# Two-block layer on one core: one feed-forward round in pairs of units over four PSUM banks, and one unit half in products of 256 columns

## The chip, the cores and the metric

One Trainium2 chip; the program uses 1 of its cores. The metric is the device time of the whole kernel in microseconds, one launch. The kernel before took 1955.97 us (median of 3 runs, 1955.89 to 1957.13).

## The reference

The input `x` is 512 tokens of 1024 numbers. It passes through two blocks. The first has sparse attention beside a linear recurrence and a gated feed-forward part. The second has two layers; what a layer of it computes at its end is what the change touches:

```python
for l in range(DEPTH_2):                                  # 2 layers
    ...
    x = x + jnp.einsum('bse,ed->bsd', mixed, w_o[l])
    h = rmsnorm(x, mlp_norm[l])
    u = jnp.square(jax.nn.relu(jnp.einsum('bsd,df->bsf', h, w_ff1[l])))   # 1024 -> 4096
    x = x + jnp.einsum('bsf,fd->bsd', u, w_ff2[l])                        # 4096 -> 1024
return rmsnorm(x, final_norm)
```

All tensors are float32.

## The kernel before, in words

Activations lie transposed in SBUF: 8 tiles of 128 features by 512 tokens. A matrix product with a weight is cut into **units**: a unit makes 128 output features for all 512 tokens, in one PSUM bank, from 8 tiles of 128 input features. To keep the accuracy of float32 with the faster float32r products, weights and activations are each split into a high and a low part, and each of the 8 steps `k` is three products of 512 columns: high weight by high activation, high weight by low activation, low weight by high activation (L1621, L1622, L1623). A unit is therefore 24 products, each with a weight load of its own. 280 units of the kernel run in this form, numbered through; unit n uses bank `accs[n % 2]`.

The program is one list of items (`whole()`), and every engine walks the same list and does its own part of each item, in the order of the list. What happens for unit n:

- SyncE starts the load of its 512 KB into `raw` (L671), one of 3 slots, as soon as the unit that had the slot has been split.
- ScalarE makes the high part with one copy of 128 x 1024 (`split_hi`, L778). It does so two units ahead: in the item `mmA` of unit n it splits unit n + 2.
- GpSimd makes the low part in 4 pieces of 128 x 256 (`split_lo`, L737). It waits for the high part and then runs as early as it may. `whi` and `wlo` are rings of 4 slots.
- TensorE has two items for a unit, `mmA` (k 0 to 3) and `mmB` (k 4 to 7). `mmA` waits for the high part, for half of the low part, and for the accumulator to be free (semaphore `acc`: every unit up to n - 2 has been read); `mmB` waits for the rest of the low part.
- VectorE reads the finished bank. In a unit of the first weight (`w_ff1`) this is the item `relu`: VectorE multiplies the bank by the norm (L1105), makes relu and square (L1458), ScalarE copies the result to its high part `Uh` (L1013), VectorE makes the low part `Ul` (L1461). In a unit of the second weight (`w_ff2`) it is `resid`: one VectorE addition into `xT` (L1210).

The feed-forward part of a layer of the second block runs in 4 rounds of 1024 hidden features, `ffn_round(r, last)`: 8 units of `w_ff1`, each followed by its `relu`, then 8 units of `w_ff2`, each followed by its `resid`. The first unit of `w_ff2` waits for `Ul` tile by tile (`first`). In layer 0 round 0 is units 135 to 150, **round 1 is units 151 to 166**, round 2 is units 167 to 182.

The wait on the accumulator and the order of ScalarE's work are these lines:

```python
if begun("unit", -1):
    pe.wait_ge(sems["acc"], at("unit", -1))      # mmA of unit n: units 0 to n - 2 were read
...
for ahead in item[1].get("splits", (2,)):        # ScalarE, mmA of unit n
    split_hi(ahead)
```

Of the kernel before, what the change touches and what calls it, by code (L numbers as in the profile page):

```python
# [52 lines left out]
def shape_constants():  # L53
# [43 lines left out]
    "xin": dict(S_fill=1, S_act=1, xh=1, xl=1), "xsq": dict(), "xsum": dict(x_sum=1), "warm": dict(), "split": dict(), "loads": dict(), "cmpc": dict(cmp_c=1),  # L97
    "prep": dict(sq=1, xh=1, xl=1),
    "norm": dict(M_fill=1, M_act=1, rstd=1), "norm0": dict(M_fill=1, M_act=1, rstd=1),
    "mmA": dict(), "mmB": dict(unit=1), "mmK": dict(),  # L100
    "resid": dict(acc=1),

    "evc": dict(acc=1, cmp_t=1),
# [132 lines left out]
def mm(unit):  # L236
    return [("mmA", unit), ("mmB", unit)]
# [171 lines left out]
def block2(layer, behind=0):  # L409
    s = [("lay",)]  # L410

    def u(col, **kw):
        return unit("w_in_2", col, "h", k0=8 * layer, **kw)

    cols = {"sq": 0, "sk": 512, "sv": 1024, "dq": 1536, "dk": 2048, "dv": 2560}
    attn = []
    for kind, j, *rest in periods(ORDER2, LAST2):
        if kind in ("mmA", "mmB"):
            begins = j == 0 and rest[0] == "sq"
            attn.append((kind, u(cols[rest[0]] + 128 * j, first=begins)))  # L420
            if begins and kind == "mmB":
                attn.append(("norm",))
        elif kind == "on2":
            attn.append(("on2", j, 4 + j))
        elif kind in ("vt", "vt2", "dfr", "rope"):
            attn.append((kind, *rest))
        else:
            attn.append((kind, j, *rest))
    order = produced(attn)
    w_o = [unit("w_o_2", 128 * c, "u", order, first=(c < 4), k0=8 * layer, bank=c) for c in range(KC)]  # L430
    attn = with_early(attn, w_o)
    s += attn
    s += outputs(w_o, attn, "cur", 8)

    def ffn_round(r, last):
        out = []
        for c in range(8):
            out += mm(unit("w_ff1_2", 1024 * r + 128 * c, "h", first=(c == 0 and r == 0), k0=8 * layer))
            out += ([("norm",)] if c == 0 and r == 0 else []) + [("relu", c)]
        for c in range(KC):  # L440
            out += mm(unit("w_ff2_2", 128 * c, "u", first=(c == 0), k0=32 * layer + 8 * r)) + [("resid", c)]
            if last:
                out.append(("prep", c, ("cur", c)))
        return out

    s += ffn_round(0, False) + ffn_round(1, False)
    if layer == 0:
        return s + ffn_round(2, False) + ffn_round(3, True)
    s += [("gload",)] + ffn_round(2, False)
    last = units_of(s) + behind + 8  # L450

    def down(n):
        return unit("w_ff2_2", P * ((last + n) % RING if n < RING else n), "u", k0=32 * layer + 24)

    for c in range(8):
        s += mm(unit("w_ff1_2", 3072 + 128 * c, "h", k0=8 * layer, splits={5: (2, 3), 6: (3,), 7: (3,)}.get(c, (2,))))
        if c == 7:
            s.append(("wn", down(0), 0))
        s.append(("relu", c))
        s += [("nat", c)] if c < 6 else [("nat", 6), ("nat", 7)] if c == 7 else []  # L460
    s += [("wn", down(n), n) for n in range(1, 8)]
    s += [("grp", b, 0) for b in range(NB)]
    for b in range(NB):
        s += [("grp", b, 1), ("fin", b)]
    return s
# [49 lines left out]
def build(nc, dram, out):  # L515
    sched = whole()
    with ExitStack() as ctx:
# [129 lines left out]
        def _(sp):  # L647
# [30 lines left out]
            def stage(w, item):  # L678
# [17 lines left out]
                elif kind == "loads":  # L696
                    n = item[1]
                    if n == 0:
                        sp.dma_start(cst[:, EARLY:LATE], dram["consts"][:, EARLY:LATE]).then_inc(sems["ld_const2"], 16)
                    v, a = sems[f"ld_cmp{n}"], "kv"[n]  # L700
                    sp.dma_start(w1[n], dram[f"cmp_{a}_w1"][0].rearrange("(a p) c -> p a c", p=P)).then_inc(v, 16)
                    sp.dma_start(w2[n], dram[f"cmp_{a}_w2"][0]).then_inc(v, 16)
                elif kind == "mmA":
                    fetch(item[1], 0)
                elif kind == "mmP" and item[3] == 0:
                    fetch(item[1], item[2])
                elif kind == "rotary":
                    c0 = CONST_AT["cos"][0]
                    sp.wait_ge(sems["T_fill"], at("T_fill"))
                    sp.wait_ge(sems["S_fill"], at("S_fill"))  # L710
                    sp.dma_start(cst[:, c0:c0 + 2 * T], dram["consts"][:, c0:c0 + 2 * T]).then_inc(sems["ld_rotary"], 16)
                elif kind == "gload":
                    sp.wait_ge(sems["acc"], at("acc", -20))
                    g = dram["final_norm_2"]
                    sp.dma_start(gainT, bass.AP(g.tensor, g.offset, [[0, P], [1, D]])).then_inc(sems["ld_gain"], 16)
                elif kind == "wn":
                    fetch(item[1], item[2])
                elif kind == "fin":
                    b = item[1]
                    for h, y in enumerate(("y0", "y1")):  # L720
                        sp.wait_ge(sems[y], b + 1)
                        sp.dma_start(x_out[:, b, T * h:T * h + T], ob[:, b, T * h:T * h + T]).then_inc(sems["outd"], 16)
# [6 lines left out]
        def _(pool):  # L729
# [16 lines left out]
            def stage(w, item):  # L746
                if item[0] == "mmA":
                    split_lo(0)
                elif item[0] == "mmP" and item[3] == 0:
                    split_lo(item[2])  # L750
                elif item[0] == "wn":
# [15 lines left out]
        def _(act):  # L767
# [16 lines left out]
            def stage(w, item):  # L784
# [36 lines left out]
                elif kind == "mmA":  # L821
                    for ahead in item[1].get("splits", (2,)):
                        split_hi(ahead)
                elif kind == "mmP":
                    if item[3] == 0 and item[2] < 2:
                        split_hi(2 + item[2])
# [262 lines left out]
        def _(dve):  # L1089
# [4 lines left out]
            def acc():  # L1094
                return accs[:, (w.base["unit"] - 1) % 2]

            def gain(where):
                kind, n = where
                return vec[:, n:n + 1] if kind == "vec" else cur[:, n:n + 1]
# [22 lines left out]
            def stage(w, item):  # L1122
# [82 lines left out]
                    STT(Xl[:, c], xT[:, c], gain(g), Xh[:, c].bitcast(F32), ALU.mult, ALU.subtract).then_inc(sems["xl"], 1)  # L1205
                elif kind == "resid":
                    c = item[1]
                    dve.wait_ge(sems["unit"], at("unit"))
                    y = M[:, :] if item[2:] and item[2] == IN_M else TT[:, item[2] - 2] if item[2:] and item[2] > 1 else acc()
                    TTn(xT[:, c], xT[:, c], y, ALU.add).then_inc(sems["acc"], 1)  # L1210
                    dve.wait_ge(sems["acc"], at("acc", 1))
                elif kind == "evc":
# [241 lines left out]
                    TTn(Ul[:, item[1]], tu, Uh[:, item[1]].bitcast(F32), ALU.subtract).then_inc(sems["ul"], 1)  # L1454
                    dve.wait_ge(sems["ul"], at("ul", 1))
                elif kind == "relu":
                    scaled(tg)
                    STT(tu, tg, 0.0, tg, ALU.max, ALU.mult).then_inc(sems["u_new"], 1)  # L1458
                    dve.wait_ge(sems["u_new"], at("u_new", 1))
                    dve.wait_ge(sems["uh"], at("uh", 1))  # L1460
# [90 lines left out]
        def _(pe):  # L1551
# [10 lines left out]
            def stage(w, item):  # L1562
# [41 lines left out]
                elif kind in ("mmA", "mmB"):  # L1604
# [10 lines left out]
                    for i, k in enumerate(ks):  # L1615
# [2 lines left out]
                        if u["first"]:  # L1618
                            pe.wait_ge(sems[ready], at(ready, i + 1 - len(ks) + u.get("early", 0)))
                        y = accs[:, n % 2]  # L1620
                        mmul(y, whi[:, slot, k], xh[:, k], start=(i == 0), stop=False)  # L1621
                        mmul(y, whi[:, slot, k], xl[:, k], start=False, stop=False)  # L1622
                        last = mmul(y, wlo[:, slot, k], xh[:, k], start=False, stop=(i == len(ks) - 1))  # L1623
                    if kind == "mmB":
                        last.then_inc(sems["unit"], 1)
                elif kind == "mmP":
                    _, u, ahead, lo, hi = item
                    n = w.base.get("unit", 0) + ahead
# [301 lines left out]
```

## Time and profile before

| | |
|---|---|
| median of 3 runs | 1955.97 us |
| profiled execution, first to last instruction (its own time: no other is recorded) | 1953.9 us |
| median less that span | 2.1 us |
| TensorE busy with products | 1923.8 us, 98% |
| TensorE weight loads (they run beside products) | 1510.5 us, 77% |
| VectorE busy | 916.7 us, 47% |
| ScalarE busy | 834.5 us, 43% |
| GpSimd busy | 881.6 us, 45% |
| mean granted TensorE clock | 0.999 of full speed |
| DMA | 86 GB/s in the mean |

The span is the time from the first to the last instruction of the profiled execution. The busy time of products counts each from its start to its modelled end, 0.39 us for 512 columns, so that neighbours overlap; what one product costs is the distance between two starts, called the pitch here.

### The profile page before, as it was taken

To read this page: it belongs to the slowest core of one execution; us is meant where nothing else is said; L and a number is where in the kernel's file an instruction comes from. 1 tells how busy PE (TensorE), PEld (TensorE's weight loads), DVE (VectorE), ACT (ScalarE), POOL (GpSimd) and SP (SyncE) were. 2 spreads that over 40 slices of the span, in tenths; PEclk is the share of its full clock that TensorE was granted. 3 is DMA by queue.
4 is the path that set the end of the run, shared out by engine and by line. 5 is a ranking of instruction groups with operands and counts; after the bars stand their busy time and mean duration, and the time that the engine had idled before them with its cause. 6 is when DMAs were issued, how large, how long until landed. Compare 5 with 4: busy or idle time off the path is not lost. (4 is left out here: it accounts for less than half of the span.)

```text
span 1953.9 us, 25592 instructions
## 1 busy us (share of the span) xinstructions
PE 1923.8 (98%) x9150; PEld 1510.5 (77%) x9150; DVE 916.7 (47%) x1420; ACT 834.5 (43%) x1269; POOL 881.6 (45%) x1188
## 2 busy tenths in 40 slices
PE   9999999999999999999999999999999999999998
PEld 7866766788888887777688888887777688888887
DVE  5487877432241346777541313133777643222132
ACT  4466555543242345555532223134555542222233
POOL 4322221456456465343355455454443355454543
PEclk9999999999999999999999999999999999999999
DMA  8211111233234233222134233333222223243322
GB/s 234 65 44 44 34 44 33 87 106 110 84 89 119 76 96 99 75 66 75 48 107 116 78 108 97 87 97 95 78 66 76 65 85 110 86 119 86 109 86 76
DMA packets 318100, 168.77 MB, mean 86 GB/s; under 512 B 15028, under 2 KB 313367, under 8 KB 317847
## 3 DMA queue, kind: packets, MB, share of 16 engines
q1 hardware_dynamic: 314432, 162.38, 28.9%
q10 hardware_dynamic: 3542, 4.76, 1.0%
q8 instruction: 74, 1.21, 0.3%
q14 instruction: 52, 0.42, 0.1%
HBM read 160.29 MB, written 2.10 MB: 83 GB/s over the span
## 5 line engine op out<-in xcount | busy, mean ns | idle before, releaser
L737 POOL TENSOR_TENSOR wlo<-raw,whi 128x256 fp32r<-128x256 f32 x1164 | 865.2, 775 | 1042.2 <-ACT whi L778 1042.2
L1621 PE MATMUL accs<-Xh,whi 128*128 128x512 f32 x1448 | 581.3, 401 | 0.1
L1623 PE MATMUL accs<-Xh,wlo 128*128 128x512 f32 x1448 | 565.1, 390 | 0.0
L1622 PE MATMUL accs<-Xl,whi 128*128 128x512 f32 x1448 | 563.9, 389 | 0.0
L778 ACT ACTIVATE whi<-raw 128x1024 fp32r<-128x1024 f32 x291 | 307.7, 1061 | 267.6 <-PE accs L1623 218.5
L1621 PEld LDWEIGHTS accs<-Xh,whi 128*128 128x128 f32 x1448 | 272.1, 188 | 58.6 <-issue 3.7
L1623 PEld LDWEIGHTS accs<-Xh,wlo 128*128 128x128 f32 x1448 | 271.8, 188 | 58.4
L1622 PEld LDWEIGHTS accs<-Xl,whi 128*128 128x128 f32 x1448 | 272.4, 188 | 56.1 <-issue 3.6
L1621 PE MATMUL accs<-Uh,whi 128*128 128x512 f32 x744 | 289.7, 389 | 0.8 <-DVE xT L1210 0.8
L1622 PE MATMUL accs<-Ul,whi 128*128 128x512 f32 x744 | 289.4, 389 | 0.0
L1623 PE MATMUL accs<-Uh,wlo 128*128 128x512 f32 x744 | 289.4, 389 | 0.0
L1210 DVE TENSOR_TENSOR xT<-xT,accs 128x512 f32<-128x512 f32 x101 | 69.4, 687 | 338.1 <-PE accs L1623 333.9
L1105 DVE TENSOR_TENSOR W<-accs,rstd 128x512 f32<-128x512 f32 x123 | 85.1, 692 | 261.8 <-PE accs L1623 244.0
L1013 ACT ACTIVATE Uh<-W 128x512 fp32r<-128x512 f32 x86 | 54.4, 632 | 313.8 <-DVE W L1458 272.0
L1621 PEld LDWEIGHTS accs<-Uh,whi 128*128 128x128 f32 x744 | 139.7, 188 | 30.9 <-issue 1.6
L1623 PEld LDWEIGHTS accs<-Uh,wlo 128*128 128x128 f32 x744 | 139.7, 188 | 29.1
L1622 PEld LDWEIGHTS accs<-Ul,whi 128*128 128x128 f32 x744 | 139.7, 188 | 28.7
L1461 DVE TENSOR_TENSOR Ul<-W,Uh 128x512 fp32r<-128x512 f32 x64 | 45.1, 705 | 49.3 <-ACT Uh L1013 49.3
L1510 DVE TENSOR_TENSOR_SCAN W<-W 128x128 f32<-128x128 f32 (+3 forms) x64 | 58.3, 910 | 3.1 <-ACT W L1029 0.9
L836 ACT ACTIVATE sq<-xT 128x512 f32<-128x512 f32 x40 | 25.4, 634 | 78.8 <-DVE xT L1210 72.5
L1001 ACT ACTIVATE W<-W 128x512 f32<-128x512 f32 x22 | 13.9, 633 | 102.0 <-DVE W L1110 102.0
L1458 DVE SCALAR_TENSOR_TENSOR W<-W 128x512 f32<-128x512 f32 x64 | 47.2, 738 | 2.2
(303 smaller groups left out, 1913.8 us busy)
## 6 DMA issues: line engine op xcount, KB each, us to landing
raw<-in_w_ff_dram SPq DMA_DIRECT2D x128, 512.0 KB
raw<-in_w_in_dram SPq DMA_DIRECT2D x71, 512.0 KB
raw<-in_w_gate_up_dram SPq DMA_DIRECT2D x44, 512.0 KB
raw<-in_w_down_dram SPq DMA_DIRECT2D x16, 512.0 KB
raw<-in_w_o_dram SPq DMA_DIRECT2D x16, 512.0 KB
px<-W ACTq DMA_DIRECT2D x64, 64.0 KB, 2.0
raw<-in_w_down_dram SPq DMA_DIRECT2D x8, 384.0 KB
W<-in_x_dram SPq DMA_DIRECT2D x4, 512.0 KB, 6.1
```

What stands on the lines that cost most here:

```text
L737: pool.tensor_tensor(lo[:, ks], raw[:, unit_no % RAW, ks], hi[:, ks].bitcast(F32), ALU.subtract).then_inc(sems["wlo"], 1)
L778: A(XhW[:, ahead - RING] if ahead >= RING and late else whi[:, slot], raw[:, n % RAW], ACT.Copy).then_inc(sems["whi"], 1)
L836: A(sq[:, :], xT[:, c], ACT.Square).then_inc(sems["sq"], 1)
L1013: A(Uh[:, c], tu, ACT.Copy).then_inc(sems["uh"], 1)
L1105: TTn(dst, accs[:, (w.base["unit"] - 1 - back) % 2], rstd[:, :], ALU.mult).then_inc(sems["acc"], 1)
L1210: TTn(xT[:, c], xT[:, c], y, ALU.add).then_inc(sems["acc"], 1)
L1458: STT(tu, tg, 0.0, tg, ALU.max, ALU.mult).then_inc(sems["u_new"], 1)
L1461: TTn(Ul[:, item[1]], tu, Uh[:, item[1]].bitcast(F32), ALU.subtract).then_inc(sems["ul"], 1)
L1510: dve.tensor_tensor_scan(back, back, backwards(R[:, h, :]), 0.0, ALU.add, ALU.add).then_inc(sems["dve"], 1)
L1621: mmul(y, whi[:, slot, k], xh[:, k], start=(i == 0), stop=False)
L1622: mmul(y, whi[:, slot, k], xl[:, k], start=False, stop=False)
L1623: last = mmul(y, wlo[:, slot, k], xh[:, k], start=False, stop=(i == len(ks) - 1))
```

## The change

1. `ffn_round` gets an argument `woven`; it is true for round 1 of layer 0 only. In that round two units are one item `mm2`. Its products alternate: step k of unit n, step k of unit n + 1, for each of the three kinds of product. The units of the round take four banks in turn, `accs[0]`, `accs[1]`, `S[0]`, `S[1]` (unit n has bank n % 4); `S` belongs to the attention and lies idle here. The two `relu` or `resid` of a pair follow both units in the list.
2. An `mm2` waits at its start for the high and low parts of both units, and for `acc` up to unit n - 3 (two pairs back); the first pair of the round waits until all units before it were read.
3. In an `mm2`, SyncE fetches both units, ScalarE splits the units n + 2 and n + 3, and GpSimd makes the low parts of n and n + 1.
4. In round 2 of layer 0, unit 170 (c = 3) runs its steps k 4 to 7 as `mmH`: each product of 512 columns becomes two of 256 columns into the two halves of the same bank, each with its own weight load.

```diff
-    def ffn_round(r, last):
+    def ffn_round(r, last, woven=False):
         out = []
+        if woven:
+            for c in range(0, 8, 2):
+                out.append(("mm2", unit("w_ff1_2", 1024 * r + 128 * c, "h", k0=8 * layer),
+                            unit("w_ff1_2", 1024 * r + 128 * c + 128, "h", k0=8 * layer), c == 0))
+                out += [("relu", c, 1), ("relu", c + 1, 0)]
+            for c in range(0, KC, 2):
+                out.append(("mm2", unit("w_ff2_2", 128 * c, "u", first=(c == 0), k0=32 * layer + 8 * r),
+                            unit("w_ff2_2", 128 * c + 128, "u", first=(c == 0), k0=32 * layer + 8 * r), False))
+                out += [("resid", c, 0, 1), ("resid", c + 1, 0, 0)]
+            return out
         for c in range(8):
-            out += mm(unit("w_ff1_2", 1024 * r + 128 * c, "h", first=(c == 0 and r == 0), k0=8 * layer))
+            u = unit("w_ff1_2", 1024 * r + 128 * c, "h", first=(c == 0 and r == 0), k0=8 * layer)
+            if r == 2 and c == 3 and layer == 0:
+                u["loose"] = True
+            out += [("mmA", u), ("mmH", u)] if r == 2 and c == 3 and layer == 0 else mm(u)
...
-    s += ffn_round(0, False) + ffn_round(1, False)
+    s += ffn_round(0, False) + ffn_round(1, False, layer == 0)
...
+                elif kind == "mm2":                      # SyncE
+                    fetch(item[1], 0)
+                    fetch(item[2], 1)
...
+                elif item[0] == "mm2":                   # GpSimd
+                    split_lo(0)
+                    split_lo(1)
...
+                elif kind == "mm2":                      # ScalarE
+                    split_hi(2)
+                    split_hi(3)
...
+            def bank4(n):                                # VectorE
+                return (accs[:, 0], accs[:, 1], S[:, 0], S[:, 1])[n % 4]
...
                 elif kind == "resid":
                     c = item[1]
-                    dve.wait_ge(sems["unit"], at("unit"))
-                    y = M[:, :] if item[2:] and item[2] == IN_M else TT[:, item[2] - 2] if item[2:] and item[2] > 1 else acc()
+                    back = item[3] if item[3:] else 0
+                    dve.wait_ge(sems["unit"], at("unit", -back))
+                    y = bank4(at("unit", -1 - back)) if item[3:] else M[:, :] if item[2:] and item[2] == IN_M else TT[:, item[2] - 2] if item[2:] and item[2] > 1 else acc()
...
                 elif kind == "relu":
-                    scaled(tg)
+                    if item[2:]:
+                        dve.wait_ge(sems["unit"], at("unit", -item[2]))
+                        dve.wait_ge(sems["rstd"], at("rstd"))
+                        TTn(tg, bank4(at("unit", -1 - item[2])), rstd[:, :], ALU.mult).then_inc(sems["acc"], 1)
+                        dve.wait_ge(sems["acc"], at("acc", 1))
+                    else:
+                        scaled(tg)
...
+                elif kind == "mm2":                      # TensorE
+                    _, u, u1, begins = item
+                    n = w.base["unit"]
+                    banks = (accs[:, 0], accs[:, 1], S[:, 0], S[:, 1])
+                    pe.wait_ge(sems["whi"], n + 2)
+                    pe.wait_ge(sems["wlo"], LO_PARTS * (n + 2))
+                    pe.wait_ge(sems["acc"], n if begins else n - 2)
+                    pe.wait_ge(sems["S_act"], at("S_act"))
+                    pe.wait_ge(sems["S_dve"], at("S_dve"))
+                    xh, xl, ready = (Xh, Xl, "xl") if u["x"] == "h" else (Uh, Ul, "ul")
+                    for k in range(KC):
+                        if u["first"]:
+                            pe.wait_ge(sems[ready], at(ready, k + 1 - KC))
+                        for a in range(2):
+                            mmul(banks[(n + a) % 4], whi[:, (n + a) % RING, k], xh[:, k], start=(k == 0), stop=False)
+                        for a in range(2):
+                            mmul(banks[(n + a) % 4], whi[:, (n + a) % RING, k], xl[:, k], start=False, stop=False)
+                        for a in range(2):
+                            last = mmul(banks[(n + a) % 4], wlo[:, (n + a) % RING, k], xh[:, k], start=False, stop=(k == KC - 1))
+                            if k == KC - 1:
+                                last.then_inc(sems["unit"], 1)
+                elif kind == "mmH":
+                    u = item[1]
+                    n = w.base["unit"]
+                    slot = n % RING
+                    pe.wait_ge(sems["wlo"], LO_PARTS * (n + 1))
+                    for k in range(KC // 2, KC):
+                        for h in range(2):
+                            t = slice(T // 2 * h, T // 2 * h + T // 2)
+                            y = accs[:, n % 2, t]
+                            mmul(y, whi[:, slot, k], Xh[:, k, t], start=False, stop=False, skip_group_check=True)
+                            mmul(y, whi[:, slot, k], Xl[:, k, t], start=False, stop=False, skip_group_check=True)
+                            last = mmul(y, wlo[:, slot, k], Xh[:, k, t], start=False, stop=(k == KC - 1), skip_group_check=True)
+                    last.then_inc(sems["unit"], 1)
```

The first place is ScalarE at the start of round 1: `whi<-raw` is the high part of a weight (L778, L797 in the change), `Uh<-W` the copy in a `relu` (L1013, L1035 in the change). Before:

```order
L1013 ACTIVATE Uh<-W 128x512
L778 ACTIVATE whi<-raw 128x1024 x9
L1013 ACTIVATE Uh<-W 128x512
L778 ACTIVATE whi<-raw 128x1024
L1013 ACTIVATE Uh<-W 128x512
```

And in the change:

```order
L1035 ACTIVATE Uh<-W 128x512
L797 ACTIVATE whi<-raw 128x1024 x10
L1035 ACTIVATE Uh<-W 128x512 x2
L797 ACTIVATE whi<-raw 128x1024 x2
L1035 ACTIVATE Uh<-W 128x512 x2
```

One high part after each `relu` became two high parts after each two `relu`: behind the `relu` of the first pair (units 151, 152) stand the high parts of units 155 and 156.

The second place is TensorE at the same point of the program, from the last step of unit 150 to the second step of the pair 151 and 152. Before:

```order
L1623 MATMUL accs<-Uh,wlo 128x512
L1621 MATMUL accs<-Xh,whi 128x512
L1622 MATMUL accs<-Xl,whi 128x512
L1623 MATMUL accs<-Xh,wlo 128x512
L1621 MATMUL accs<-Xh,whi 128x512
```

And in the change, where lines L1673, L1675 and L1677 are the three products of `mm2`:

```order
L1656 MATMUL accs<-Uh,wlo 128x512
L1673 MATMUL S<-Xh,whi 128x512
L1673 MATMUL accs<-Xh,whi 128x512
L1675 MATMUL S<-Xl,whi 128x512
L1675 MATMUL accs<-Xl,whi 128x512
L1677 MATMUL S<-Xh,wlo 128x512
L1677 MATMUL accs<-Xh,wlo 128x512
L1673 MATMUL S<-Xh,whi 128x512
```

The number of products of the round is the same, 384; each is now followed by one into another bank. Of this pair, unit 151 goes to `S[1]` and unit 152 to `accs[0]`, the bank of unit 150.

## Rows read from the trace of the kernel before

**Rows 1.** The page: span, and busy time and instructions of each engine

```profile
span 1953.9 us, 25592 instructions
PE 1923.8 (98%) x9150; PEld 1510.5 (77%) x9150; DVE 916.7 (47%) x1420; ACT 834.5 (43%) x1269; POOL 881.6 (45%) x1188
```

**Rows 2.** Round 1: stretch, busy PE, PEld, DVE, ACT, POOL, clock, DMA share, GB/s

```profile
1078.30:1165.30 87.00, 87.00 (x386) 72.06 (x385) 22.12 (x32) 21.95 (x24) 45.13 (x64) 1.00 0.34 97
```

**Rows 3.** Timeline of TensorE (start us, us): from unit 150 into unit 151

```profile
1078.17 0.39 PE L1623 MATMUL accs<-Uh,wlo 128*128 128x512 f32 x1
1078.40 0.39 PE L1621 MATMUL accs<-Xh,whi 128*128 128x512 f32 x1
...
1078.40 0.19 PEld L1622 LDWEIGHTS accs<-Xl,whi 128*128 128x128 f32 x1
```

**Rows 4.** Timeline of TensorE: a change of bank in the attention of layer 1

```profile
1552.40 0.40 PE L1648 MATMUL accs<-Uh,wlo 128*128 128x512 f32 x1
1552.63 0.40 PE L1646 MATMUL TT<-Uh,whi 128*128 128x512 f32 x1
```

**Rows 5.** Timeline of VectorE: last `resid` of round 0, first `relu` of round 1

```profile
1078.67 0.69 DVE L1210 TENSOR_TENSOR xT<-xT,accs 128x512 f32<-128x512 f32 x1 [4.75 <-PE accs L1623]
1084.10 0.69 DVE L1105 TENSOR_TENSOR W<-accs,rstd 128x512 f32<-128x512 f32 x1 [4.74 <-PE accs L1623]
1084.82 0.69 DVE L1458 SCALAR_TENSOR_TENSOR W<-W 128x512 f32<-128x512 f32 x1
1086.28 0.69 DVE L1461 TENSOR_TENSOR Ul<-W,Uh 128x512 fp32r<-128x512 f32 x1 [0.77 <-ACT Uh L1013]
```

**Rows 6.** Timeline of ScalarE in round 1

```profile
1085.54 0.63 ACT L1013 ACTIVATE Uh<-W 128x512 fp32r<-128x512 f32 x1 [11.32 <-DVE W L1458]
1086.21 1.06 ACT L778 ACTIVATE whi<-raw 128x1024 fp32r<-128x1024 f32 x1
...
1124.29 2.01 ACT L778 ACTIVATE whi<-raw 128x1024 fp32r<-128x1024 f32 x2
```

**Rows 7.** Timeline of GpSimd in round 1

```profile
1087.35 2.83 POOL L737 TENSOR_TENSOR wlo<-raw,whi 128x256 fp32r<-128x256 f32 x4 [10.23 <-ACT whi L778]
1125.43 8.40 POOL L737 TENSOR_TENSOR wlo<-raw,whi 128x256 fp32r<-128x256 f32 x12 [2.61 <-ACT whi L778]
```

**Rows 8.** Timeline: TensorE held by VectorE's read of a bank, layer 1

```profile
1565.27 1.41 DVE L1210 TENSOR_TENSOR xT<-xT,accs 128x512 f32<-128x512 f32 x2 [1.12 <-PE accs L1648]
...
1566.94 0.47 PE L1621 MATMUL accs<-Uh,whi 128*128 128x512 f32 x1 [0.39 <-DVE xT L1210]
1567.25 0.40 PE L1622 MATMUL accs<-Ul,whi 128*128 128x512 f32 x1
```

**Rows 9.** Timeline: TensorE held by a high part, after eight transposes

```profile
1902.72 1.03 PE L1559 MATMUL S<-cst,xT 128*128 128x128 f32 x8
1902.92 1.06 ACT L778 ACTIVATE whi<-raw 128x1024 fp32r<-128x1024 f32 x1 [1.69 <-PE accs L1623]
...
1904.03 0.50 PE L1897 MATMUL accs<-whi,Uh 128*128 128x512 f32 x1 [0.28 <-ACT whi L778]
```

**Rows 10.** Timeline of round 0: VectorE and GpSimd at the same time

```profile
1003.22 1.18 DVE L1458 SCALAR_TENSOR_TENSOR W<-W 128x512 f32<-128x512 f32 x1
1001.72 3.28 POOL L737 TENSOR_TENSOR wlo<-raw,whi 128x256 fp32r<-128x256 f32 x4 [4.97 <-ACT whi L778]
```

**Rows 11.** A weight's DMA in round 1: its issue; stretches with the columns of rows 2

```profile
1090.26 5.83 SPq L671 DMA_DIRECT2D raw<-in_w_ff_dram  x2
...
1090.20:1091.20 1.00, 1.00 (x6) 0.84 (x5) 0.72 (x2) 0.21 (x1) 0.00 (x0) 1.00 0.00 0
1091.20:1093.80 2.60, 2.60 (x13) 2.15 (x12) 0.69 (x1) 1.48 (x2) 1.01 (x2) 1.00 0.70 201
```

**Rows 12.** Groups by form (count | busy us, mean ns of one | idle): transposes, products of 64 rows

```profile
L1559 PE MATMUL S<-cst,xT 128*128 128x128 f32 x32 | 4.6, 272 | 0.0
L1854 PE MATMUL TT<-W 64*128 64x512 f32 x32 | 9.0, 641 | 0.0
```

More of the change, by code:

```diff
@@ L99 @@
     "norm": dict(M_fill=1, M_act=1, rstd=1), "norm0": dict(M_fill=1, M_act=1, rstd=1),
-    "mmA": dict(), "mmB": dict(unit=1), "mmK": dict(),
+    "mmA": dict(), "mmB": dict(unit=1), "mmK": dict(), "mm2": dict(unit=2), "mmH": dict(unit=1),
     "resid": dict(acc=1),
@@ L1620, in stage @@
                         y = accs[:, n % 2]
-                        mmul(y, whi[:, slot, k], xh[:, k], start=(i == 0), stop=False)
-                        mmul(y, whi[:, slot, k], xl[:, k], start=False, stop=False)
-                        last = mmul(y, wlo[:, slot, k], xh[:, k], start=False, stop=(i == len(ks) - 1))
+                        loose = "loose" in u
+                        mmul(y, whi[:, slot, k], xh[:, k], start=(i == 0), stop=False, skip_group_check=loose)
+                        mmul(y, whi[:, slot, k], xl[:, k], start=False, stop=False, skip_group_check=loose)
@@ L1624, in stage @@
+                        last = mmul(y, wlo[:, slot, k], xh[:, k], start=False, stop=(i == len(ks) - 1), skip_group_check=loose)
                     if kind == "mmB":
                         last.then_inc(sems["unit"], 1)
+                elif kind == "mm2":
[32 more added lines that the diff above has]
+                    last.then_inc(sems["unit"], 1)
```

## The prediction

> **What bounds the kernel now.** I read the page first. TensorE has products under way in 98% of the span, while VectorE, ScalarE and GpSimd stay below 48% [rows 1]. Then the busy time by stretch: in round 1 of layer 0, units 151 to 166, TensorE has no idle time at all in 87.0 us, at the full clock, and DVE, ACT and POOL are busy for 22, 22 and 45 us of it [rows 2]. So in the stretch that the change touches every delay of TensorE goes into the total, and the work of the other engines matters only where TensorE comes to wait for it. Nothing later gives a delay back: the kernel is bound by TensorE to its end. The timeline gives the pitch. The last product of unit 150 starts at 1078.17 and the first of unit 151 at 1078.40, 0.23 us later [rows 3]. Over the round it is finer: 386 products touch the stretch of 87.00 us, and as one lasts 0.39 us, two of them began before it [rows 2, 3]. 87.00 / 384 = 0.2266 us for a product, 5.44 us for a unit of 24 and 10.88 us for a pair of units; VectorE's reads of units 150 and 151 agree, 1078.67 and 1084.10 [rows 5]. A product of 512 columns at 2.4 GHz would be 0.2133 us, so 0.0133 us come on top.
>
> **The change, part by part.** The number of products of round 1 stays 384, and so do its weight loads, VectorE and ScalarE instructions, GpSimd pieces and DMAs. What changes is the bank that follows on a bank, what TensorE waits for, and when.
>
> *1. Alternating banks: 0.* The trace has full-height products that change bank. Unit 150 to unit 151 is `accs[0]` to `accs[1]`, 0.23 us [rows 3]; `accs` to `TT` is 0.23 us as well [rows 4]. No saving is seen at a change of bank, so I take 0.227 us for all 384. The Trainium skill, "TensorE: Matmul & The Clock Gate", section "Back-to-back issue gap", gives columns over 2.4 GHz plus 2.5 ns when warm, 0.2158 us here; the trace disagrees by 0.011 us per product, and if the new order came down to the page's figure the round would win an estimated 4.2 us.
>
> *2. Entry into the round: +1.2 us.* Units 151 and 152 go to `S[1]` and `accs[0]`, and `accs[0]` holds unit 150. The first pair therefore waits until VectorE has added unit 150. That addition starts 0.50 us after the start of the unit's last product and takes 0.69 us, to 1079.36 [rows 3, 5]. From there to the first product it takes 0.05 us at least (ScalarE ends at 1903.98, the product starts at 1904.03 [rows 9]) and 0.26 us at most (VectorE's additions end at 1566.68, the product starts at 1566.94 [rows 8]). Here two more waits follow the one that holds, so I take 0.2: start at 1079.56 where it was 1078.40, 1.16 us. The product after a stop follows 0.31 us behind it, not 0.23 [rows 8]: 0.08 more. Together 1.24 us.
>
> *3. The low part of the pair after next: +1.2 us, twice.* Write L for the start of the last product of a pair of `w_ff1`. The first unit's last product is one pitch earlier, so VectorE begins its `relu` at L + 0.27. One `relu` lasts 2.87 us to the end of `Ul` (1084.10 to 1086.97) and 2.07 us to the end of `Uh` (1086.17) [rows 5, 6]. The second starts at L + 3.17 and its `Uh` is copied at L + 5.24. Only then, in ScalarE's order, come the two high parts, which in the kernel before stood one behind each `relu`; they are 2.01 us together, the first 1.06 [rows 6], so they end at L + 6.34 and L + 7.29. GpSimd starts 0.08 us after a high part (1087.27 to 1087.35) and needs 8.40 / 12 = 0.70 us a piece [rows 6, 7]: 8 pieces end at L + 12.02. A pair of products waits for all 8 at its start, where before the first unit would have waited for its own first half alone. With 0.2 us to the first product it begins at L + 12.22. TensorE, meanwhile, does the next pair and would be ready at L + 0.23 + 10.88 = L + 11.11. It waits 1.11 us, with the slow second product 1.19 us. The low parts of the first two pairs come out of the old order in time, so the third pair of the round is the first that waits. The delay puts the next pair's low part (counted from the end of the second pair) level with TensorE, so waits fall on every other pair: on the third pair and the fifth, the first of `w_ff2`. 2 x 1.19 = 2.38 us. From the sixth pair on no `relu` stands ahead of the high parts; the low parts are then done about 7 us after the pair before last and nothing waits. The sixth pair itself still follows the fourth's `relu` and is level.
>
> *4. The level pairs: +0.15 us, twice.* For the fourth and sixth pairs TensorE is ready at L + 0.23 + 10.65 + 0.08 + 12.22 = L + 23.18 and the low part at L + 10.88 + 12.22 = L + 23.10, with L of the first pair (or third). VectorE's L1458 would then begin at L + 10.88 + 0.99 while GpSimd still works until L + 12.02, an overlap of 0.15 us. Where the two overlap the first takes 1.18 us in place of 0.69 and the four pieces 3.28 in place of 2.83 [rows 5, 7, 10]; I count the overlap as lost once. That makes L + 23.25, 0.07 us late, and 0.08 for the restart. 0.30 us for both; 0 if they just miss.
>
> *5. Exit: +0.9 us.* Unit 167 is again in `accs[1]`, the bank of unit 165, which ended one pitch before the end of the round. VectorE's addition is done at 0.27 + 0.69 = 0.96 us after the last product's start and no further wait follows, so TensorE starts at 1.01 in place of 0.23, and 0.08: 0.86 us. The second `resid` of the other pairs delays nobody, because four banks are in turn.
>
> *6. Unit 170 in halves: +0.2 us.* 12 products of 512 columns, 2.72 us, become 24 of 256. At 2.4 GHz that is 0.1067 us, and with the same 0.0133 us on top 0.120 us, if the weight load hides. Eight transposes with eight loads of 128 x 128 take 1.03 us, of which the last is 0.27 [rows 9, 12], so loads follow each other every (1.03 - 0.27) / 7 = 0.109 us and keep up with 0.120. 24 x 0.120 = 2.88, +0.16 us. Bounds: 0, half of the 512-column pitch; and +1.8 us, if each product had to wait for a whole load of 0.19 us [rows 3], 24 x 0.19 = 4.56. The Trainium skill, "TensorE: Matmul & The Clock Gate", section "The mechanism" of its Part 3, says that a load overlaps a running product only in another row group. By that rule an estimated 0.107 us of load would be added to each half product and the unit would cost 2.7 us more. The trace speaks against it: the load for L1622 starts at 1078.40, together with the product L1621, in all rows of the array.
>
> *7. DMA: 0.* A weight is issued at 1090.26, when its slot is free, moves between 1091.2 and 1093.8 and is there after 3.6 us [rows 7, 11]. The slot of the second weight of a pair is free when the first half of GpSimd's 8 pieces is done, L + 9.3, and landed at L + 12.9; ScalarE wants it 6.3 us after the next pair's end, L + 17.2. It has 4 us to spare.
>
> Sum: 1.24 + 2.38 + 0.30 + 0.86 + 0.16 = **4.9 us**. The profiled span of 1953.9 us would become 1958.8 us. The median of the runs, 1955.97 us, lies 2.1 us above that span, and I add the same 4.9 us: **1960.9 us**.
>
> **The rivals.**
>
> *The pitch falls between banks, and the round breaks even.* If what each product has on top of its columns came from writing the bank that the last one wrote, the 384 products would win up to 384 x 0.0133 = 5.1 us, and 1955.8 us would be left of 1960.9. For it: the kernel never alternates for long. Against it: the single changes of bank [rows 3, 4]. Down to the page's floor it would be 1956.7 us.
>
> *Two banks take two products at once: faster.* The trace has products that go to two banks in turn and overlap: 32 of 64 rows, 0.64 us each, fill only 9.0 us, 0.28 us for each [rows 12], so that each covers more of the next than the full-height ones do (0.23 of 0.39 us). They use the two halves of the array. If full-height products in two banks overlapped by only a tenth of a pitch, 384 x 0.0227 = 8.7 us would be won, 1952.2 us. It decides from a mean pitch of 0.2266 - 4.9 / 384 = 0.214 us downward, and shows a gain above noise only below 0.204, less than the columns take. Full-height products share all rows of the array, so I give it little.
>
> *No wait on the low parts.* If the 2.01 us or the 5.6 us were shorter, or the second `relu` did not hold ScalarE, parts 3 and 4 would go and 2.3 us remain: 1958.2 us. Each of the three durations is a row, none can shrink by 1.1 us.
>
> *More waits than counted.* If the level pairs miss by as much as the others (2 x 1.0 us more) or the half products wait for their loads (1.7 us), it would be 1962.5 to 1964.6 us.
>
> **How the numbers follow.** A measurement of this kernel tells a change of about 0.2%, 3.9 us. The forecast, waits and nothing won, with terms between 4.1 us (each start at 0.05 us, level pairs free) and 5.5 us (each start at 0.26 us, level pairs later by 0.2 us each), has 0.74. More waits has 0.11, no wait on the low parts 0.06, break even 0.06, overlapping products 0.03. The range from 1959.2 to 1963.4 us holds the forecast with the spread of the runs before (1.2 us) and half of the case above. Slower by over 0.2%, which begins at 1959.9: most of the forecast and all above it, 0.79. Within 0.2%: 0.17. Faster: 0.04.
>
> **What would show it.** In the profile after, products L1673 to L1677 at a pitch of 0.227 us; TensorE idle about 0.8 us before the first of them with VectorE's `resid` as releaser; two stops of about 1 us after GpSimd's L753 before the third and fifth pair, none before the seventh and eighth; one stop before unit 167; half products every 0.12 us. The prediction is wrong if the pitch in the round is below 0.22 us, if the stops are missing, or if a DMA is what ends one of them.

## The result, and the profile after

The changed kernel takes 1960.43 us (median of 11 runs, 1959.79 to 1962.73), the kernel before, measured beside it, 1955.89 us (11 runs, 1955.11 to 1957.75). The ratio is 1.0022, with a 95% interval of 1.0014 to 1.0031: 4.5 us slower, 1960.9 us were predicted. The profiled execution took 1960.48 us and its span is 1958.7 us, 4.8 us over [rows 1]; 1958.8 us was predicted. Runs of one kernel differ by 3 us and more, and one trace of the experiments shows where such time can go: in the profiled run of the kernel with other banks (below), 1962.93 us where its median is 1957.97, the mean granted clock was 0.86 from 1525 to 1550 us, far from the round, and 1.00 in the round.

The page of the kernel after, against [rows 1]:

```profile
span 1958.7 us, 25619 instructions
PE 1925.8 (98%) x9162; PEld 1510.9 (77%) x9162; DVE 916.2 (47%) x1420; ACT 834.0 (43%) x1269; POOL 883.0 (45%) x1188
```

Nearly all is as before; TensorE has 12 products more (unit 170), and the busy shares say nothing of 4.8 us. The busy time by stretch does, against [rows 2] (stretch, length, PE, PEld, DVE, ACT, POOL, clock, DMA share, GB/s):

```profile
1079.60:1170.00 90.40, 88.00 (x384) 71.67 (x384) 21.51 (x32) 20.13 (x24) 42.06 (x60) 1.00 0.32 91
```

The stretch runs from just before the first product of the woven round to just before the first of unit 167. The same 384 products lie in 90.40 us, not 87.0, and TensorE is idle for 2.4 us of it; one more idle time, of 1.0 us, lies just before it. The timeline of TensorE shows four stops of about a microsecond, at the entry, before the third and fifth pair, and at the exit (the number in brackets is the idle time before a product, counted from the modelled end of the one before):

```profile
1078.22 0.39 PE L1656 MATMUL accs<-Uh,wlo 128*128 128x512 f32 x1
1079.62 0.47 PE L1673 MATMUL S<-Xh,whi 128*128 128x512 f32 x1 [1.01 <-issue]
1079.92 0.39 PE L1673 MATMUL accs<-Xh,whi 128*128 128x512 f32 x1
1080.15 0.39 PE L1675 MATMUL S<-Xl,whi 128*128 128x512 f32 x1
...
1101.23 0.39 PE L1677 MATMUL S<-Xh,wlo 128*128 128x512 f32 x1
1102.53 0.47 PE L1673 MATMUL S<-Xh,whi 128*128 128x512 f32 x1 [0.91 <-issue]
1102.83 0.40 PE L1673 MATMUL accs<-Xh,whi 128*128 128x512 f32 x1
...
1124.27 0.39 PE L1677 MATMUL S<-Xh,wlo 128*128 128x512 f32 x1
1125.49 0.47 PE L1673 MATMUL S<-Uh,whi 128*128 128x512 f32 x1 [0.84 <-issue]
1125.81 0.39 PE L1673 MATMUL accs<-Uh,whi 128*128 128x512 f32 x1
...
1168.98 0.39 PE L1677 MATMUL S<-Uh,wlo 128*128 128x512 f32 x1
1170.08 0.47 PE L1654 MATMUL accs<-Xh,whi 128*128 128x512 f32 x1 [0.72 <-DVE xT L1236]
1170.39 0.40 PE L1655 MATMUL accs<-Xl,whi 128*128 128x512 f32 x1
```

For three of the four the profile names no engine as releaser, only "issue"; an `mm2` has several waits in a row there. Who ended such a stop has to be read from the other engines. VectorE's read of unit 150, and GpSimd's low parts (the second row is the low part of the third pair, the third that of the fourth, the fourth that of the fifth):

```profile
1078.71 0.69 DVE L1236 TENSOR_TENSOR xT<-xT,accs 128x512 f32<-128x512 f32 x1 [4.75 <-PE accs L1656]
```

```profile
1096.83 5.59 POOL L753 TENSOR_TENSOR wlo<-raw,whi 128x256 fp32r<-128x256 f32 x8 [14.23 <-ACT whi L797]
1107.78 5.60 POOL L753 TENSOR_TENSOR wlo<-raw,whi 128x256 fp32r<-128x256 f32 x8 [5.36 <-ACT whi L797]
1119.79 5.61 POOL L753 TENSOR_TENSOR wlo<-raw,whi 128x256 fp32r<-128x256 f32 x8 [6.40 <-ACT whi L797]
```

GpSimd ends at 1102.42 and TensorE starts at 1102.53; it ends at 1125.40 and TensorE starts at 1125.49. In both cases the second ScalarE copy of a `relu` stands before the high parts; for the third pair the rows are:

```profile
1092.06 0.63 ACT L1035 ACTIVATE Uh<-W 128x512 fp32r<-128x512 f32 x1 [12.36 <-DVE W L1490]
1095.03 0.63 ACT L1035 ACTIVATE Uh<-W 128x512 fp32r<-128x512 f32 x1 [2.34 <-DVE W L1490]
1095.69 2.01 ACT L797 ACTIVATE whi<-raw 128x1024 fp32r<-128x1024 f32 x2
```

Taken from the starts of the products, in us over the pitch of 0.227, the slower second product included:

| stop | predicted | measured |
|---|---|---|
| entry | 1.24 | 1.25 |
| third pair | 1.19 | 1.15 |
| fourth pair | 0.15 | 0.03 |
| fifth pair | 1.19 | 1.09 |
| sixth pair | 0.15 | 0.07 |
| exit | 0.86 | 0.96 |
| unit 170 | 0.16 | 0.17 |
| sum | 4.9 | 4.7 |

Of the other products of the round, a few in the first two microseconds behind a stop take 0.232 to 0.236 us; all the rest follow their predecessor after 0.227 us, as before.

The half of unit 170 in 256 columns begins with these rows, and the next unit's products follow it:

```profile
1189.21 0.28 PE L1689 MATMUL accs<-Xh,whi 128*128 128x256 f32 x1
1189.33 0.28 PE L1690 MATMUL accs<-Xl,whi 128*128 128x256 f32 x1
1189.44 0.28 PE L1691 MATMUL accs<-Xh,wlo 128*128 128x256 f32 x1
...
1192.08 0.40 PE L1654 MATMUL accs<-Xh,whi 128*128 128x512 f32 x1
1192.32 0.40 PE L1655 MATMUL accs<-Xl,whi 128*128 128x512 f32 x1
```

By the starts in ns, the second product comes 0.113 us behind the first, and all later ones 0.119 to 0.120 us apart; their weight loads settle at 0.120 us too. The two products of 512 columns behind them take 0.234 and 0.235 us.

### The profile page after: what moved, and what is told of

It reads as the page before. It is cut to its first block and busy times, and to the rows that moved or that the text cites. A ratio compares the mean times of both kernels' runs of the same rounds, so it can differ in the third digit from the quotient of the medians.

```text
span 1958.7 us, 25619 instructions
## 1 busy us (share of the span) xinstructions
PE 1925.8 (98%) x9162; PEld 1510.9 (77%) x9162; DVE 916.2 (47%) x1420; ACT 834.0 (43%) x1269; POOL 883.0 (45%) x1188
## 5 line engine op out<-in xcount | busy, mean ns | idle before, releaser
L1654 PE MATMUL accs<-Xh,whi 128*128 128x512 f32 x1380 | 554.9, 402 | 0.8 <-DVE xT L1236 0.7
L1656 PE MATMUL accs<-Xh,wlo 128*128 128x512 f32 x1380 | 538.7, 390 | 0.0
L1655 PE MATMUL accs<-Xl,whi 128*128 128x512 f32 x1380 | 537.5, 389 | 0.0
L797 ACT ACTIVATE whi<-raw 128x1024 fp32r<-128x1024 f32 x291 | 307.0, 1060 | 275.7 <-PE accs L1656 195.2
L1654 PEld LDWEIGHTS accs<-Xh,whi 128*128 128x128 f32 x1380 | 259.3, 188 | 56.8 <-issue 4.8
L1656 PEld LDWEIGHTS accs<-Xh,wlo 128*128 128x128 f32 x1380 | 259.0, 188 | 55.7
L1655 PEld LDWEIGHTS accs<-Xl,whi 128*128 128x128 f32 x1380 | 259.6, 188 | 53.7 <-issue 3.6
L1654 PE MATMUL accs<-Uh,whi 128*128 128x512 f32 x680 | 264.8, 389 | 0.8 <-DVE xT L1236 0.8
L1656 PE MATMUL accs<-Uh,wlo 128*128 128x512 f32 x680 | 264.5, 389 | 0.0
L1655 PE MATMUL accs<-Ul,whi 128*128 128x512 f32 x680 | 264.5, 389 | 0.0
L1035 ACT ACTIVATE Uh<-W 128x512 fp32r<-128x512 f32 x86 | 54.4, 632 | 311.1 <-DVE W L1490 269.4
L1654 PEld LDWEIGHTS accs<-Uh,whi 128*128 128x128 f32 x680 | 127.6, 188 | 28.3 <-issue 1.6
L1490 DVE SCALAR_TENSOR_TENSOR W<-W 128x512 f32<-128x512 f32 x64 | 47.4, 740 | 2.2
```

Of the source, the lines that this page charges most:

```text
L797: A(XhW[:, ahead - RING] if ahead >= RING and late else whi[:, slot], raw[:, n % RAW], ACT.Copy).then_inc(sems["whi"], 1)
L1035: A(Uh[:, c], tu, ACT.Copy).then_inc(sems["uh"], 1)
L1655: mmul(y, whi[:, slot, k], xl[:, k], start=False, stop=False, skip_group_check=loose)
```

## The experiments

All have the kernel before as reference, measured on the same chip. Its median is 1955.61 us beside the woven round alone, the other banks, ScalarE's order and the two together; 1956.09 us beside TensorE's wait, both layers, unit 170 alone and the products of 128 columns; and 1956.62 us beside the many halves and the products of 384. Differences are between medians; the ratio with its 95% interval was worked out from the single runs and can differ from that of the medians by 0.0003.

**Does the table add up: the woven round alone.** Unit 170 is left as before:

```diff
-            out += [("mmA", u), ("mmH", u)] if r == 2 and c == 3 and layer == 0 else mm(u)
+            out += mm(u)
```

> The woven round alone, unit 170 as before. Stops add up (theory): the five stops of TensorE in the round, 1.25 + 1.15 + 0.04 + 1.09 + 0.07 + 0.96 us as the profile after shows them at entry, third, fourth, fifth and sixth pair and exit, make +4.5 us. Rival, the half products cost more than their place in the profile shows: below +4 us.

Measured: 1960.14 us, +4.5 us, ratio 1.0023 (1.0014 to 1.0032). The six stops (the list above has six, though it says five) sum to 4.6 us in its profile; those of the fourth and sixth pair are 0.07 and 0.10 us here. The round is the whole of it, as far as runs can tell.

**Entry and exit: another order of banks.**

```diff
-                return (accs[:, 0], accs[:, 1], S[:, 0], S[:, 1])[n % 4]
+                return (accs[:, 0], accs[:, 1], S[:, 0], S[:, 1])[(n + 2) % 4]
...
-                    banks = (accs[:, 0], accs[:, 1], S[:, 0], S[:, 1])
+                    banks = (S[:, 0], S[:, 1], accs[:, 0], accs[:, 1])
...
-                    pe.wait_ge(sems["acc"], n if begins else n - 2)
+                    pe.wait_ge(sems["acc"], n - 1 if begins else n - 2)
```

and unit 167, whose bank the last pair no longer uses, waits for one read less.

> The woven round with its four banks turned by two (unit 151 in accs[1], 152 in S[0], the last two in S[1] and accs[0]), so that the first pair needs no read of unit 150 and unit 167 none of the pair before it; unit 170 as before. Stops add up: entry and exit go (1.25 + 0.96), +2.3 us left. Rival, the stop only moves: a later wait takes the 2.2 us back, +4.5 us.

Measured: 1957.97 us, +2.4 us, ratio 1.0010 (1.0001 to 1.0019). The stops at entry and exit are gone and the one before the third pair is where it was:

```profile
1101.30 0.39 PE L1677 MATMUL accs<-Xh,wlo 128*128 128x512 f32 x1
1102.59 0.47 PE L1673 MATMUL accs<-Xh,whi 128*128 128x512 f32 x1 [0.90 <-issue]
```

The stops left in the round sum to 2.3 us. The rival, a wait that only moves, is out. The stops at entry and exit went with one edit, so this run does not part them; each has its own row and releaser in the profile after.

**The stops between: ScalarE's order.** The high parts of units n + 2 and n + 3 are made ahead of the two `relu` copies, as soon as their slots come free; the flag `item[4]` leaves them in the `mm2` for the first pair of `w_ff1` and for the pairs of `w_ff2` from the second on, which have no `relu` ahead:

```diff
                 elif kind in ("up", "relu"):
                     c = item[1]
+                    if item[2:] and item[2] == 1:
+                        split_hi(2)
+                        split_hi(3)
...
-                elif kind == "mm2":
+                elif kind == "mm2" and item[4]:
                     split_hi(2)
                     split_hi(3)
```

> The woven round with the two high parts of the pair after next made ahead of the two relu copies in ScalarE's order; unit 170 as before. Theory (the order on ScalarE holds GpSimd back): the stops at the third to sixth pair go, low parts done at about L + 7.2 instead of L + 12.0, +2.2 us left. Rival (GpSimd's 8 pieces, or the later relu copies, bound the pair): stops of about 1 us stay at every other pair, +4.5 us.

Measured: 1957.76 us, +2.2 us, ratio 1.0010 (1.0002 to 1.0019). Its ScalarE and GpSimd at the same place as above:

```profile
1091.00 2.01 ACT L795 ACTIVATE whi<-raw 128x1024 fp32r<-128x1024 f32 x2 [10.88 <-PE S L1678]
1092.92 0.61 ACT L1036 ACTIVATE Uh<-W 128x512 fp32r<-128x512 f32 x1
```

```profile
1092.14 7.16 POOL L751 TENSOR_TENSOR wlo<-raw,whi 128x256 fp32r<-128x256 f32 x8 [9.13 <-ACT whi L795]
```

GpSimd begins 1.3 us after the start of the pair's last product (L in the prediction), where it was 6.5 us. It now works beside VectorE's `relu` and needs 7.16 us where it needed 5.59, so that it ends at L + 8.5 and not at the L + 7.2 that was expected. At 1099.30 it still is 2.6 us ahead of TensorE, which starts the third pair at 1101.91. No stop is left between the pairs, and the rival is out.

**The same stops, taken away at the other end: TensorE's wait.** ScalarE's order stays as in the change; the wait on the low parts is spread over the products that read them:

```diff
-                    pe.wait_ge(sems["wlo"], LO_PARTS * (n + 2))
...
+                        if k % 2 == 0:
+                            pe.wait_ge(sems["wlo"], LO_PARTS * (n + 1) + k // 2 + 1)
                         for a in range(2):
                             last = mmul(banks[(n + a) % 4], wlo[:, (n + a) % RING, k], xh[:, k], start=False, stop=(k == KC - 1))
```

> The woven round with the wait on the low parts spread: a pair starts on its high parts and waits for each quarter of the second unit's low part just before the first product that reads it; ScalarE's order stays as in the change, unit 170 as before. Theory (TensorE is held only because it wants all 8 pieces at the start): stops at the third to sixth pair go, +2.2 us left. Rival (the high parts or the slots are late as well): a stop of 0.3 us or more stays at the third and fifth pair.

Measured: 1958.14 us, +2.1 us, ratio 1.0009 (1.0000 to 1.0018). GpSimd is as late as in the change, and the third pair does not stop:

```profile
1096.65 5.61 POOL L751 TENSOR_TENSOR wlo<-raw,whi 128x256 fp32r<-128x256 f32 x8 [14.15 <-ACT whi L795]
```

```profile
1101.05 0.39 PE L1676 MATMUL S<-Xh,wlo 128*128 128x512 f32 x1
1101.28 0.39 PE L1670 MATMUL S<-Xh,whi 128*128 128x512 f32 x1
1101.51 0.39 PE L1670 MATMUL accs<-Xh,whi 128*128 128x512 f32 x1
```

The pair starts at 1101.28, 1.0 us before GpSimd is done at 1102.26. So the high parts and the slots were in time, and the rival is out; both halves of the cause (the order on ScalarE, and the wait for all pieces) are needed for a stop.

**No stop left: what the alternation itself is worth.** Both the other banks and the other order on ScalarE.

> Both: banks turned and high parts ahead of the relu copies; unit 170 as before. Theory (alternating banks neither win nor cost): no stop is left, all 384 products at 0.227 us, same as before within 0.3 us. Rival (alternating banks win at the changes, hidden by the stops): faster than before by up to 5 us. Rival (stops come back elsewhere): +1 us or more.

Measured: 1956.03 us, +0.4 us between the medians, ratio 0.9999 (0.9990 to 1.0007), which is no change. Its round and its first products:

```profile
1079.01:1166.01 87.00, 87.00 (x385) 72.10 (x384) 24.25 (x31) 19.75 (x23) 48.27 (x60) 1.00 0.33 97
```

```profile
1079.01 0.39 PE L1676 MATMUL accs<-Xh,whi 128*128 128x512 f32 x1
1079.24 0.39 PE L1676 MATMUL S<-Xh,whi 128*128 128x512 f32 x1
1079.47 0.39 PE L1678 MATMUL accs<-Xl,whi 128*128 128x512 f32 x1
```

384 products in two banks alternately take the 87.0 us of [rows 2]; the pitch between starts is 0.2267 us. This settles the rival of the falling pitch: it is neither there nor hidden by stops. No gap between two products of the round is over 0.228 us, so no stop came back elsewhere in it.

**Is there slack elsewhere: the woven round in both layers.** `ffn_round(1, False, True)`, unit 170 as before.

> The woven round in both layers of the second block, unit 170 as before. Theory (TensorE bound throughout, each stop goes into the total): twice the +4.5 us, +9.1 us. Rival (layer 1 has slack, or other banks meet there): clearly off 9.1, below 7 or above 11 us.

Measured: 1965.03 us (5 runs), +8.9 us, ratio 1.0047 (1.0034 to 1.0059). Both rounds have the same stops to 0.001 us, with a sum of 4.6 us each. A microsecond of TensorE in this round is a microsecond of the kernel in either layer.

**Unit 170 alone.** `ffn_round(1, False)` and the rest of the change.

> Unit 170 half in products of 256 columns, no woven round: +0.17 us by the profile after (2.87 us where 2.72 us stood, and slower neighbours), which the runs can't tell from no change; 24 products 0.120 us apart.

Measured: 1955.62 us, ratio 1.0001 (0.9992 to 1.0010). The runs can't see it. In its profile the half takes 2.87 us, as in the profile after.

**Many halves, to see it.** In rounds 1 to 3 of layer 0 all 24 units of `w_ff1` take their second half in 256 columns, and no round is woven:

```diff
-            if r == 2 and c == 3 and layer == 0:
+            if r > 0 and layer == 0:
                 u["loose"] = True
-            out += [("mmA", u), ("mmH", u)] if r == 2 and c == 3 and layer == 0 else mm(u)
+            out += [("mmA", u), ("mmH", u)] if r > 0 and layer == 0 else mm(u)
```

> No woven round; in rounds 1 to 3 of layer 0 all 24 units of w_ff1 have their second half in products of 256 columns. If a half in 256 columns costs the 0.17 us that the profile after shows for one (0.120 us per product and slower neighbours), +4.1 us. Rival (the 0.120 us is paid once and later products go at half the pitch of 512 columns, 0.1135 us): +0.4 us or less.

Measured: 1960.82 us, +4.2 us, ratio 1.0023 (1.0014 to 1.0032). In its profile each of the 24 halves takes 2.873 us from its first product to the next unit's, 0.15 us over 2.72, or 3.7 us for all; the slower products behind them add 0.03 us each, 0.7 us for all. The rival, paid once, is out. In each of the 24 halves the second product comes 0.113 to 0.114 us behind the first.

**Why 0.120 us: products of 128 columns.**

```diff
-                        for h in range(2):
-                            t = slice(T // 2 * h, T // 2 * h + T // 2)
+                        for h in range(4):
+                            t = slice(T // 4 * h, T // 4 * h + T // 4)
```

> Unit 170 half in products of 128 columns, 48 of them, no woven round. Theory A, that of the prediction (each product has 0.0133 us on top of its columns at 2.4 GHz, loads hide): 0.067 us apart, 3.2 us, +0.5 us. Theory B (at 256 columns it is already the weight load that sets 0.120 us): 0.12 us apart, 5.8 us, +3.0 us.

Measured: 1958.10 us, +2.0 us, ratio 1.0012 (1.0004 to 1.0021). By its profile the half takes 5.31 us in place of 2.72, +2.6 us, which the interval of the runs holds:

```profile
1184.36 0.22 PE L1689 MATMUL accs<-Xh,whi 128*128 128x128 f32 x1
1184.42 0.28 PE L1690 MATMUL accs<-Xl,whi 128*128 128x128 f32 x1
1184.53 0.27 PE L1691 MATMUL accs<-Xh,wlo 128*128 128x128 f32 x1
1184.65 0.27 PE L1689 MATMUL accs<-Xh,whi 128*128 128x128 f32 x1
```

```profile
1184.14 0.19 PEld L1689 LDWEIGHTS accs<-Xh,whi 128*128 128x128 f32 x1
1184.37 0.19 PEld L1690 LDWEIGHTS accs<-Xl,whi 128*128 128x128 f32 x1
1184.47 0.19 PEld L1691 LDWEIGHTS accs<-Xh,wlo 128*128 128x128 f32 x1
1184.59 0.19 PEld L1689 LDWEIGHTS accs<-Xh,whi 128*128 128x128 f32 x1
```

Neither theory holds as written. The first product of 128 columns has its successor 0.057 us behind (0.06 in the rows); that successor's load had started as the first product did, so one short product costs 0.057 us. All others are 0.109 to 0.115 us apart, 0.112 in the mean, and their loads an even 0.112. A is out: 0.067 us appears nowhere. The even spacing of the loads, at twice what the first product costs, speaks for B, in which the load decides at 128 columns, but at 0.112 us, not 0.12.

**And of 384 and 128 columns.** The slices are `(0, 384)` and `(384, 512)`.

> No woven round; unit 170's second half in products of 384 and 128 columns, 12 of each. If what a product has on top grows with its columns (0.227 / 512 = 0.000443 us a column), a product of 384 takes 0.170 us; if it is a fixed 0.0133 us, 0.173 us. The product of 128 behind it: 0.111 us or more if its successor's load decides, 0.057 us if not; in the first case the half costs 12 x 0.281 = 3.4 us, +0.7 us, in the second 2.7 us, no change.

Measured: one run, 1958.47 us, which alone says nothing of half a microsecond; its profile is what counts:

```profile
1184.50 0.33 PE L1688 MATMUL accs<-Xh,whi 128*128 128x384 f32 x1
1184.67 0.34 PE L1689 MATMUL accs<-Xl,whi 128*128 128x384 f32 x1
1184.85 0.34 PE L1690 MATMUL accs<-Xh,wlo 128*128 128x384 f32 x1
1185.02 0.23 PE L1688 MATMUL accs<-Xh,whi 128*128 128x128 f32 x1
1185.08 0.28 PE L1689 MATMUL accs<-Xl,whi 128*128 128x128 f32 x1
1185.19 0.27 PE L1690 MATMUL accs<-Xh,wlo 128*128 128x128 f32 x1
```

The first product of 384 columns takes 0.171 us to its successor, the next two 0.175 and 0.177 us. The first one of 128 columns takes 0.06 us, the two after it 0.11 us. The first of each length fits a cost that goes with the columns, though 0.171 lies only 0.002 us from the fixed sum, and it is 128 and 256 columns (0.057 for 0.067 us, 0.113 for 0.120) that part the two. The loads hold the short products behind the first. The half takes 3.40 us, the 3.4 us of the first case, +0.7 us; the first long product after the short ones takes 0.23 us, in place of 0.17.

## Why the prediction was right

*The view that carried it.* A stretch in which TensorE has no idle time at all [rows 2] turns the question into a count of its stops. The time came within 0.5 us, and the losses lie at the six places where they were put: behind VectorE at entry and exit, behind GpSimd at the pairs between. The terms are right to 0.12 us each and their sum to 0.2 us; the rest of the 0.5 us lies within the spread of the runs. The experiments show these causes by taking them away; entry and exit go with the banks, the others with ScalarE's order or with TensorE's wait, and all together with both.

*Part 1, alternation 0.* Right, and the one part on which the sign hung. Two rows with a change of bank [rows 3, 4] spoke for the other 384; the run with both edits has them without a stop, at 0.2267 us. The 0.2158 us worked out from the Trainium skill ("TensorE: Matmul & The Clock Gate", "Back-to-back issue gap") is what that section gives for an isolated product, beside 131 ns at 512 columns for a stream of loads and products. Neither is met in either order; the traces have 226.7 ns.

*Parts 2 and 5, entry and exit.* 1.25 and 0.96 us measured, 1.24 and 0.86 predicted. The exit was 0.1 short because 0.05 us was taken from VectorE's end to the product; it was 0.15. The idle time before the first product was given as 0.8 us; the prediction's own start at 1079.56 makes it 1.0, and the profile after has 1.01.

*Part 3, the low parts.* The chain L + 12.02 is in the profile to 0.1 us: the last product of the first pair starts at L = 1090.35, and GpSimd ends at 1102.42, L + 12.07. The start behind GpSimd took 0.10 us, not the 0.2 that was taken between the bounds of 0.05 and 0.26.

*Part 4, the level pairs.* That the two are level was right and the size was too large, 0.03 and 0.07 us for 0.15 each. The first product of either pair started on the pitch, at 1113.53 and 1136.46, 0.15 and 0.12 us behind GpSimd's end; only the second product was late. The shorter start behind GpSimd leaves them level, and the clash of L1490 with GpSimd cost 0.07 us in the fourth pair's chain (0.76 us for 0.69), 0.01 in the sixth's, and not 0.15.

*Part 6, unit 170.* 0.17 us for 0.16, but the step behind it failed. It took what a product has over its columns at 2.4 GHz as a fixed 0.0133 us, and so 0.120 us for 256 columns. The first product of each row of shorter ones shows a cost in proportion to the columns: 0.057, 0.113, 0.171 and 0.227 us for 128, 256, 384 and 512 columns, 0.00044 us a column. That rests on one product each at 128 and 384 columns, on 24 at 256 and on the whole round at 512. The fixed sum holds neither at 128 columns nor for the first product of 256, so that the 0.120 us of the other 256-column products met it is, as far as the runs show, chance. Why it is 0.120 us, above both the 0.1135 us of half a product and the 0.112 us of the load, stays open; the short products behind one another, and also the first long ones behind them (0.234 us), run a little slower than either limit. The rule on row groups in the Trainium skill ("TensorE: Matmul & The Clock Gate", Part 3, "The mechanism") would have made an estimated 0.227 us of it; the same section also lets a load go ahead of running products if it is into the background weight buffer. In the traces the load of the next product starts with the running one, in the same rows of the array, as [rows 3] said; which buffer it fills they do not show.

*The sum's bounds.* With each start at 0.05 us and the level pairs free the sum is 4.2 us, not 4.1; nothing hangs on it.

*The chances.* Slower by over 0.2% was given 0.79. The ratio is 1.0022, near that line, so the 0.17 for no change was not idle.

## What to carry to other kernels

When the bound engine has no gap in a stretch, pairing its work can only pay if the pitch itself falls, and here two rows at a change of bank already said that it does not. What pairing surely does is to make twice as much work fall due at one point: here the reads of two banks, then two high parts behind them in ScalarE's order, then eight pieces of low part before the first product. Wait for each piece where it is read, put what the bound engine needs next ahead of what it needs later, and look which bank the unit before a new bank order used. The first two were each enough against the stops between the pairs; the second and the third together made the pairing cost nothing, and it also won nothing.

## What the runs showed of the hardware

- Products of full height in two banks alternately have the same pitch as in one, 0.227 us for 512 columns, over 384 products.
- A product of float32r in a stream of 512 columns takes 0.443 ns a column, and the first product of a row of 128, 256 or 384 columns does too. Behind it a row of 128 columns runs at 0.112 us, as its loads do, one of 256 at 0.120 us, and products of 384 take 0.175 us.
- From the end of the releaser to the first product it took 0.10 us behind GpSimd, 0.15 behind VectorE at the exit and 0.21 at the entry, and the second product after a stop of a microsecond came 0.31 us behind the first; a few products after it took 0.232 to 0.236 us.
- GpSimd's 8 pieces took 5.6 us with VectorE idle for most of them and 7.16 us beside VectorE's two `relu`; nobody waited for the difference.
